# Three matmuls per weight tile into one PSUM half, in place of two into a whole bank

## The reference

```python
h = h + 0.5 * rmsnorm(swiglu(rmsnorm(h, gn[0]), ffn1_w_in[i], ffn1_w_out[i]), gn[1])
hn = rmsnorm(h, gn[2])
m = mixer(hn)            # hgrn2, diff_attention, pool, hgrn2; then hybrid (SSD and attention), recurrent
h = h + rmsnorm(m, gn[3])
h = h + 0.5 * rmsnorm(swiglu(rmsnorm(h, gn[4]), ffn2_w_in[i], ffn2_w_out[i]), gn[5])

def swiglu(x, w_in, w_out):
    g, u = jnp.split(x @ w_in, 2, axis=-1)      # w_in 1024 x 5632, w_out 2816 x 1024
    return (jax.nn.silu(g) * u) @ w_out
```

## Time and profile before

| what | value |
|---|---|
| median of 3 runs (lowest to highest) | 3526.33 us (3525.63 to 3526.66) |
| span of the profiled execution | 3531.6 us |
| profiled span against that median | 5.3 us longer |
| TensorE busy, mean granted clock | 91%, 0.960 |
| VectorE, ScalarE, GpSimd busy | 67%, 52%, 8% |
| HBM read over the span | 151 GB/s |

### The profile page before, as it was taken

How to read it: one execution, slowest core, us unless ns; L and a number is a source line. 1 busy time by engine, 2 the same in 40 slices (tenths; PEclk the granted TensorE clock), 3 DMA queues, 4 the chain that set the end, 5 groups by cost and what they waited for, 6 DMA issues and landing times.

```text
span 3531.6 us, 47236 instructions
## 1 busy us (share of the span) xinstructions
PE 3227.6 (91%) x17800; PEld 2755.1 (78%) x17800; DVE 2375.7 (67%) x2692; ACT 1823.6 (52%) x2180; POOL 268.6 (8%) x184
## 2 busy tenths in 40 slices
PE   8988899998699998799998899999887999997798
PEld 7876788887588887688887678888775788886687
DVE  6767676766576677576766767576765676767675
ACT  4555655554455554555555555555342555555553
POOL 1010101010000001101010010101000101010101
PEclk9998999999899999899999899999997999998899
DMA  5543355554245464355553336455440455553353
GB/s 171 198 136 108 115 183 167 178 190 131 72 157 196 153 194 138 114 179 166 178 192 119 97 130 200 147 187 167 143 155 0 131 187 170 179 191 107 109 193 127
DMA packets 527814, 534.83 MB, mean 151 GB/s; under 512 B 7817, under 2 KB 527116, under 8 KB 527688
## 3 DMA queue, kind: packets, MB, share of 16 engines
q1 hardware_dynamic: 527688, 533.08, 46.5%
HBM read 532.00 MB, written 1.05 MB: 151 GB/s over the span
## 4 chain that ended last, share of the span: by engine, by line
PE 75%; DVE 12%; ACT 9%; DVEq 3%; issue 1%; DMA 0%; SPq 0%; ACTq 0%; POOL 0%; POOLq 0%
PE pp L1992 45%; PE pp L1993 23%; DVE wlo L1826 5%; ACT whi L1718 3%; PE pm L2055 2%; ACT corr L1780 1%; DVEq L515 1%; DVE tsum L1890 0%; ACT L1795 0%; PE pm L2069 0%; DVE mix L518 0%; DVE mix L1923 0%; ACT mix L1747 0%; PE pp L1577 0%; ACT mix L730 0%
## 5 line engine op out<-in xcount | busy, mean ns | idle before, releaser
L1992 PE MATMUL pp<-xs,whi 128*128 128x512 f32 x5824 | 2101.4, 404 | 117.8 <-DVE wlo L1826 92.1
L1993 PE MATMUL pp<-xs,wlo 128*128 128x256 f32 x5824 | 1648.8, 283 | 0.0
L1992 PEld LDWEIGHTS pp<-xs,whi 128*128 128x128 f32 x5824 | 1111.4, 191 | 418.9 <-DVE wlo L1826 78.1
L1826 DVE TENSOR_TENSOR wlo<-raw,whi 128x2048 fp32r<-128x2048 f32 (+2 forms) x455 | 1114.4, 2449 | 214.4 <-ACT whi L1718 214.4
L1993 PEld LDWEIGHTS pp<-xs,wlo 128*128 128x128 f32 x5824 | 1117.4, 192 | 0.4 <-issue 0.2
L1718 ACT ACTIVATE whi<-raw 128x2048 fp32r<-128x2048 f32 (+2 forms) x455 | 926.4, 2036 | 9.0 <-DMA raw<-ffn_w_in 8.7
L1780 ACT ACTIVATE corr<-pp 128x512 f32<-128x512 f32 x468 | 279.0, 596 | 1172.8 <-PE pp L1993 1172.7
L1992 PE MATMUL pp<-hs,whi 128*128 128x512 f32 x2240 | 778.5, 392 | 8.9 <-DVE wlo L1826 7.3
L1993 PE MATMUL pp<-hs,wlo 128*128 128x256 f32 x2240 | 626.1, 280 | 0.0
L1890 DVE TENSOR_TENSOR tsum<-pp,corr 128x512 f32<-128x512 f32 x344 | 237.9, 692 | 435.9 <-ACT corr L1780 434.1
L1694 POOL TENSOR_TENSOR mix<-mix 128x256 f32<-128x256 f32 (+2 forms) x144 | 260.9, 1812 | 3232.5 <-ACT mix L1747 2869.7
(11 more groups left out here) (337 smaller groups left out, 1784.3 us busy)
## 6 DMA issues: line engine op xcount, KB each, us to landing
raw<-ffn_w_in SPq DMA_DIRECT2D x264, 1024.0 KB, 5.1
raw<-ffn_w_out SPq DMA_DIRECT2D x96, 1408.0 KB, 6.2
raw<-hgrn_w_in SPq DMA_DIRECT2D x32, 1024.0 KB, 5.4
raw<-hyb_w_in SPq DMA_DIRECT2D x24, 1024.0 KB, 5.2
raw<-diff_w_in SPq DMA_DIRECT2D x12, 1024.0 KB, 5.2
raw<-hgrn_w_out SPq DMA_DIRECT2D x8, 1024.0 KB, 5.0
raw<-hyb_w_out SPq DMA_DIRECT2D x8, 1024.0 KB, 5.0
raw<-rec_w_in SPq DMA_DIRECT2D x8, 1024.0 KB, 5.7
```

The lines of the kernel that those rows point to most:

```text
L1826: v.tensor_tensor(wlo[:, slot, 0:cols], raw[:, slot, 0:cols], whi[:, slot, 0:cols].bitcast(F32), ALU.subtract).then_inc(sem("weights_lo"), 1)
L1992: mm(bank, whi[:, slot, c:c + P], x[:, x_k, :], start=(k == 0), stop=False)
L1993: return mm(bank[:, 0:T], wlo[:, slot, c:c + P], x[:, x_k, 0:T], start=False, stop=(k == seg.kt - 1))
```

## The change

A new function `three_products` issues three matmuls of 256 columns that all add to the same 256 columns of PSUM: whi x high, whi x low, wlo x high. `tile_product` and the two block products call it. The correction half, `corr`, R_CORR and P_CORR, ScalarE's copies and VectorE's additions are removed; VectorE waits for `panel_done` itself. The multiplication by the norm factor reads PSUM and gives `panel_out`; in the `out` panels and in slot 0 of `down` it is a copy from PSUM, in slot 1 of `down` one addition. In the opening body the wait for the norm factor and the multiplication now stand ahead of the split of slot 0's next weights. The signals `gate_ready`, `hgrn_projected`, `hgrn_values`, `at_keys_in` and `at_values_in` are replaced by counts of `panel_out`. `tsum` (4 KB a partition) becomes `up` (2 KB) and `corr` (4 KB) becomes `group_rstd` (2 KB), which the hybrid mixer uses for a norm factor. The core of the diff:

```diff
 # TensorE
+            def three_products(bank, slot, c, x, first, last):
+                mm(bank, whi[:, slot, c:c + P], x[:, 0:T], start=first, stop=False)
+                mm(bank, whi[:, slot, c:c + P], x[:, T:2 * T], start=False, stop=False)
+                return mm(bank, wlo[:, slot, c:c + P], x[:, 0:T], start=False, stop=last)
             def tile_product(seg, slot, ft, x, k, x_k):
-                bank, c = pp[:, 2 * slot + ft, :], k * PC + ft * P
-                mm(bank, whi[:, slot, c:c + P], x[:, x_k, :], start=(k == 0), stop=False)
-                return mm(bank[:, 0:T], wlo[:, slot, c:c + P], x[:, x_k, 0:T], start=False, stop=(k == seg.kt - 1))
+                return three_products(pp[:, 2 * slot + ft, 0:T], slot, k * PC + ft * P, x[:, x_k, :], k == 0, k == seg.kt - 1)
 # ScalarE, read_out
                         act.wait_ge(sem("panel_done"), g + (slot + 1))
-                        nc.scalar.activation(two(corr[:, slot, :]), corr_half(slot), ACT.Copy).then_inc(sem("corr_copied"), 1)
...
-                                act.wait_ge(sem("gate_ready"), i + (f + 1))
+                                act.wait_ge(sem("panel_out"), g + 1)
 # VectorE, read_out
-                        t = two(tsum[:, slot, :])
-                        y2 = y[:, 2 * i:2 * i + 2, :] if seg.role == "down" else None
-                        if seg.role == "down" and slot == 1:
-                            dve.drain()
-                            dve.wait_ge(sem("corr_copied"), g + 2)
-                            v.tensor_tensor(y2, y2, main_half(slot), ALU.add)
-                            dve.drain()
-                            v.tensor_tensor(y2, y2, two(corr[:, slot, :]), ALU.add).then_inc(sem("panel_out"), 1)
-                        else:
-                            to = y2 if y2 is not None else t
+                        split_now = seg.role in ("down", "out")
+                        dve.wait_ge(sem("panel_done"), g + (slot + 1))
+                        if split_now:
                             if seg.role == "out":
-                                to = y[:, 4 * i + 2 * slot:4 * i + 2 * slot + 2, :]
-                            dve.wait_ge(sem("corr_copied"), g + (slot + 1))
-                            v.tensor_tensor(to, main_half(slot), two(corr[:, slot, :]), ALU.add).then_inc(sem("panel_out"), 1)
-                        wait_rstd = opening and isinstance(i, int) and i == 0 and slot == 0
-                        split_now = seg.role in ("down", "out") or wait_rstd
-                        if nxt and split_now and not (closing and i == seg.bodies - 1 and slot == 1):
-                            split(slot, g + (slot + 3), nxt)
-                        if seg.role in ("down", "out"):
+                                e = v.tensor_copy(y[:, 4 * i + 2 * slot:4 * i + 2 * slot + 2, :], main_half(slot))
+                            elif slot == 0:
+                                e = v.tensor_copy(y[:, 2 * i:2 * i + 2, :], main_half(slot))
+                            else:
+                                dve.drain()
+                                e = v.tensor_tensor(y[:, 2 * i:2 * i + 2, :], y[:, 2 * i:2 * i + 2, :], main_half(slot), ALU.add)
+                            e.then_inc(sem("panel_out"), 1)
+                            if nxt and not (closing and i == seg.bodies - 1 and slot == 1):
+                                split(slot, g + (slot + 3), nxt)
                             continue
-                        dve.drain()
-                        if wait_rstd:
+                        if opening and isinstance(i, int) and i == 0 and slot == 0:
                             dve.wait_ge(sem("rstd_ready"), 2 * s["n"] + 1)
                         if seg.role == "ffn":
                             if slot == 0:
-                                v.tensor_tensor(two(gate[:, :]), t, r2, ALU.mult).then_inc(sem("gate_ready"), 1)
+                                v.tensor_tensor(two(gate[:, :]), main_half(slot), r2, ALU.mult).then_inc(sem("panel_out"), 1)
                             else:
-                                v.tensor_tensor(t, t, r2, ALU.mult)
+                                v.tensor_tensor(two(up[:, :]), main_half(slot), r2, ALU.mult).then_inc(sem("panel_out"), 1)
...
                         if nxt and not split_now:
                             split(slot, g + (slot + 3), nxt)
 # the block products: the same edit, for the recurrent mixer
-                e = nc.scalar.activation(R_CORR[:, half, :], (pp, pm)[slot][:, :, T:2 * T], ACT.Copy)
...
-                v.tensor_tensor(dst[:, k0:k0 + 4, :], (pp, pm)[slot][:, :, 0:T], R_CORR[:, half, :], ALU.add
-                                ).then_inc(sem("rec_read" if n < 2 else "panel_out"), 1)
+                v.tensor_copy(dst[:, k0:k0 + 4, :], (pp, pm)[slot][:, :, 0:T]
+                              ).then_inc(sem("rec_read" if n < 2 else "panel_out"), 1)
```

More of the change, by code:

```diff
@@ L347, in build @@
         SECOND_ORDER = {POOL: (3, 2, 1, 0), REC: (0, 1, 2, 3)}
-        R_GATE, R_X, R_CONV, R_CORR, R_R, R_I, R_A, R_TH = (mix[:, b] for b in range(8))
+        R_GATE, R_X, R_CONV, R_R, R_I, R_A, R_TH = (mix[:, b] for b in range(7))
         def rec_dst(p):
@@ L498, in pe_rec @@
                 for k in range(k0, k0 + 4):
-                    bank = (pp, pm)[slot][:, k - k0, :]
-                    nc.tensor.matmul(bank, whi[:, slot, k * P:(k + 1) * P], xs2[:, k, :], start=True, stop=False)
-                    e = nc.tensor.matmul(bank[:, 0:T], wlo[:, slot, k * P:(k + 1) * P], xs2[:, k, 0:T], start=False, stop=True)
+                    e = three_products((pp, pm)[slot][:, k - k0, 0:T], slot, k * P, xs2[:, k, :], True, True)
                 e.then_inc(sem("rec_quarter" if n < 2 else "panel_done"), 1)
@@ L520, in dve_conv @@
             dve.drain()
-        P_U, P_W1, P_W2, P_RC, P_OUT, P_CORR = (mix[:, b] for b in range(6))
+        P_U, P_W1, P_W2, P_RC, P_OUT = (mix[:, b] for b in range(5))
         def pool_tiles(p):
@@ L541, in act_pool @@
                 act.wait_ge(sem("panel_done"), seg.g0 + slot + 1)
-                nc.scalar.activation(P_CORR[:, 4 * slot:4 * slot + 4, :], (pp, pm)[slot][:, :, T:2 * T], ACT.Copy
-                                     ).then_inc(sem("corr_copied"), 1)
                 if slot == 0:
@@ L615, in pe_pool @@
                 for n in range(4):
-                    bank = (pp, pm)[slot][:, n, :]
                     for t in range(2):
@@ L619, in pe_pool @@
                         k = 2 * (2 * slot + n // 2) + t
-                        nc.tensor.matmul(bank, whi[:, slot, c:c + P], xs2[:, k, :], start=(t == 0), stop=False)
-                        e = nc.tensor.matmul(bank[:, 0:T], wlo[:, slot, c:c + P], xs2[:, k, 0:T], start=False, stop=(t == 1))
+                        e = three_products((pp, pm)[slot][:, n, 0:T], slot, c, xs2[:, k, :], t == 0, t == 1)
                 e.then_inc(sem("panel_done"), 1)
@@ L675, in step @@
                 if name == "turn_values":
-                    pe.wait_ge(sem("at_values_in"), n)
+                    pe.wait_ge(sem("panel_out"), s["segs"][0].g0 + 3 * j + 3)
                     if j:
@@ L682, in step @@
                 elif name.startswith("scores"):
-                    pe.wait_ge(sem("at_keys_in"), n)
+                    pe.wait_ge(sem("panel_out"), s["segs"][0].g0 + 3 * j + 2)
                     if m > 1:
@@ L1130, in step @@
                 if name == "turn":
-                    pe.wait_ge(sem("hgrn_values"), n)
+                    pe.wait_ge(sem("panel_out"), s["segs"][0].g0 + 3 * j + 3)
                     if j >= 2:
@@ new lines, in body @@
+                            v.tensor_tensor(dst[slot], main_half(slot)[:, slot, :], rpre[:, :], ALU.mult).then_inc(sem("panel_out"), 1)
+                        else:
+                            turned, pairs0 = None, 0
+                            if s["kind"] == HGRN:
+                                (kind, pair), pairs0, turned = hg_panel(2 * i + slot), 4 * s["it"], "hgrn_turned"
+                            elif s["kind"] == DIFF:
+                                (kind, pair), turned = at_panel(2 * i + slot), "at_values_turned"
+                            if turned is not None and kind == "v" and pair:
+                                dve.wait_ge(sem(turned), pairs0 + pair)
+                            v.tensor_tensor(dst(2 * i + slot), main_half(slot), r2, ALU.mult).then_inc(sem("panel_out"), 1)
```

59 lines of the change are left out of this document (18 added, 41 removed).

## The result

The changed kernel takes 3567.06 us (median of 4 runs, 3565.55 to 3568.12), the one before 3526.49: the ratio is 1.011, with a 95% interval of 1.0095 to 1.0124. That is 41 us more, where 14 were forecast; it lies inside the range given and on the side forecast, but with another make-up. The profiled executions have spans of 3563.8 and 3531.6 us. Ratios compare fast executions with fast ones; one of e4 (8,173 us) and two of the kernel before that ran beside e1 to e4 (5,155 and 11,063 us) were far slower and are left out.

A forecast was written before the change was run, and what follows sets the result against it. TensorE, 91% busy, was taken as the bound, plus the places where it stands still. Terms 3 + 32 + 41 - 7 - 21 - 6 - 28 = +14 us on 3526.3 gave 3540 us, range 3505 to 3575.

The forecast's parts named there:

- Part 1: Tiles on TensorE: three 256-column slots at 0.117 us each cost about what the old pair did, about +3 us.
- Rival B: Tiles on TensorE: three loaded streams in a row settle at 0.120 us a slot, +73 us, 3613 us; chance 24%.
- Part 2: The 18 sublayer openings: the split behind the norm-factor wait restarts TensorE 2.8 us later, partly absorbed, +32 us.
- Part 3: The 18 openings: the longer TensorE gap drops the granted clock, 2.3 us lost each, +41 us.
- A: Rival at the openings: the clock holds, so its cost vanishes and the time is 3499 us; chance 10%.
- Part 4: Segment change in the FFN, 12 times: without the copy TensorE's wait for the split goes, -7 us.
- Part 5: The 18 sublayer ends: a shorter path to the square gives -21 us, fewer clock drops -6 us.
- Part 6: Inside the mixers: removing the copy and the addition gives -28 us, bounds 10 and 34.
- D: Rival in the mixers: the removed work was hidden behind other steps and gains nothing, 3568 us; chance 8%.
- C: Rival on TensorE's tiles: 256-column slots all run at 0.113 us, 3442 us; chance 11%.
- E: Rival on weight loads: the build leaves out the second load of the same weights; chance 1%.

The follow-up runs named there:

- e4: The changed kernel with 8 more clock-keeping matmuls behind each column sum, so TensorE isn't idle in the opening gap: 3537.64 us, ratio 1.0024.
- e1: The kernel before, with only the 512-column matmul cut into two of 256 in every tile but the first of a sum: 3569.37 us, ratio 1.0116.
- e7: The kernel of e2 with every tile but the first of a sum cut into six matmuls of 128 columns: 9469.64 us in one run.
- e6: The kernel of e2 with a tile's products reordered to whi x high, wlo x high, whi x low: 3502.0 us in one run.
- e2: The changed kernel with the split of slot 0's next weights put back ahead of the opening's wait for the norm factor: 3509.86 us, ratio 0.9949.
- e3: The kernel before, with only the changed kernel's opening order (norm-factor wait and multiplication ahead of slot 0's split): 3583.49 us, ratio 1.0162.
- e12: The kernel of e2 with a VectorE addition of 128x512 and its drain put back in the mixers' 80 head panels: 3538.17 us, ratio 1.0019.
- e11: The kernel of e2 with a ScalarE copy of 128x512 put back in the mixers' 80 head panels: 3536.93 us, ratio 1.0009.
- e8: The kernel of e2, but the FFN keeps two matmuls a tile, correction half, copy and addition except in its last two down panels: 3469.17 us, ratio 0.9838.

## Why the prediction came out as it did

It forecast +14 us and +41 came, +32 between the two spans. That this is inside the range is in part luck, since two misses had opposite signs: by the table the 12 FFNs came out at +63 us where the terms give some +23, and the six mixers at -30 where they give some -9. Point by point:

**Part 1, the tile, failed; it is the main miss.** "I take 0.117, the slot as it runs now." The slot of a 256-column matmul had been read between two others of 512. Three in a row take 0.120 on xs and 0.118 on hs, 0.0076 us more a tile; with 5,824 + 2,240 tiles that is 61 us of TensorE time, where 3 were forecast. e1 shows that the cut alone does it, and that it is paid in the FFNs and not in the mixers. An FFN of the changed kernel has 528 tiles, all of them cut (e1 leaves the first of each sum whole), so it pays 4.0 us, 48 in the twelve. Rival B had this (0.120, 24%) and its argument, "every stream now has a load under it, and the 512 one had room". e7 supports half of that: 128 columns still take 0.111, as if the load set a floor. It doesn't explain the rest, since 0.118 to 0.120 is above both that floor and the streaming of 256 columns. What adds it stays open. e6 excludes the order of the weights, e1 the common columns. The other engines' work is excluded too: in the trace after, xs tiles take 0.360 with VectorE and ScalarE both idle (920 tiles) and with both busy (2,049). The price of a matmul can be stated, not its cause: with the columns unchanged each one added costs 0.0071 to 0.0076 us on xs and 0.0053 to 0.0076 on hs (e2's first trace and the changed kernel's; e1 has 0.0055).

The Trainium skill's page "TensorE: Matmul & The Clock Gate" gives P / 1.2 ns for a weight load of P columns ("LDWEIGHTS (loading the stationary operand)"), by which 128 columns come to an estimate of 107 ns. The 0.111 of e7 at the full clock agrees within 4%. The 0.213 at the lower clock does not, if it is the load that sets the slot there: the slot doubles with the clock, and the formula has no clock in it. The 2.5 ns that the Trainium skill's same page has over the streaming time of a single matmul ("Back-to-back issue gap"), without a budget for its load, is a third of the 7.6 that an added one cost on xs.

**Part 2, the delay at the openings, held.** 2.8 us each were forecast and 2.76 measured in 18 openings. e3, the same order in the kernel before, costs 57 us by the ratio, 52 by the medians and 47 by the spans (delay and clock), with 32 + 41 forecast for the two. In the FFN 1.7 + 2.3 = 4.0 had been the sum; its trace has 3.0 on the mean of 11, and in the mixers 12.5 us for all six, where 12 + 14 had been summed: they hid half.

**Part 3, the clock, held in kind.** It fell behind 18 of 18 gaps. The 7 us stretches behind the openings show 42 us lost (7 x (1 - clock), summed), as forecast, but only 30 were paid by e4 and not 41, 1.7 us an opening. A, that the clock holds, falls with it. Over the whole span the loss hardly grew, from 142 to 148 us ((1 - mean clock) x span): the ends and the mixers got back nearly what the openings lost.

What parts 2 and 3 did not see is that the bank, too, now waits for the norm factor. It stays hidden behind the late split and shows only in e2, as 0.47 us an opening and a lower clock behind some.

**Part 4, the segment change, held**: the idle time ahead of the hs tiles fell by 7.8 us, 7 forecast.

**Part 5, the sublayer's end, held**: 23.2 us shorter over the 18 ends, 21 forecast, and some 3 us more up to the next start, with 6 forecast for the clock.

**Part 6, the mixers, had the right sign and too small a size.** 28 us were taken, with 34 as the upper bound. In e2's trace the mixers are 46.5 us shorter; less 4.4 for their ends (part 5) that is 42. e12 points at the step: "the addition L1890: 18 us, less 12 x 0.7, 9 remain". The chain of waits counts an addition only where it was itself the last to come. In the hybrid's stretch (2480 to 2740 us before) the chain gives 9.5% to VectorE's steps L515 and L518, and an addition that stands in such a run is paid though the chain names other lines. This is a reading and not shown: VectorE is busy for 65% of the hybrid and 73% of the recurrent mixer, and ahead of the hybrid's additions it waited 31 us for the copy, so some of them had room. 80 panels x 0.69 = 55 us would have been the bound. D, that this work was hidden, falls with e11 and e12; that its 3568 us is close to the measured time is chance.

**The sum again.** With what was measured, an FFN comes to tiles 4.0, opening's delay 2.8 less 1.1 (the second split's wait, which is gone), clock there 1.9, segment change -0.7, end -1.3 and the clock behind it -0.4: +5.2, and the table has 5.3. In the mixers the removed work (-42) and the ends (-4) are e2's -46.5, and the late split takes 17 of it back, which leaves the changed kernel's -29.7. Eleven FFNs at 5.3, the first at 4.1 and the mixers make the +32 between the two spans. The +41 between the medians is the same difference: the profiled execution of before lay 5.1 us over its median and that of the changed kernel 3.3 under its own.

C and E fell with the tiles: 0.354 and 0.360 are not 0.339, and 25,896 weight loads stand beside 25,896 matmuls.

## What to carry to other kernels

The price of a matmul slot is to be read from a run of the same slots in a row, or not taken as known: a matmul added with the columns unchanged cost up to 0.0076 us here, which is 2% of a tile, and with 528 of them in each FFN (4.0 us) it outweighed what the copy and the addition gave back there. Remove work where the engine that does it ends the waits (here the mixers and the sublayers' ends) and leave it where TensorE covers it: done in that way, and with the split kept ahead of the norm factor, the edit makes the kernel 1.6% faster instead of 1.1% slower (e8). And when an operand is read later than before, look at everything that stands behind it on that engine: moving one split behind one wait was worth 57 us, of which 30 were clock and not waiting.

## What the runs showed of the hardware

- In e7 a matmul of 128 columns in fp32r with its own weight load takes 0.111 us at the full clock and 0.213 at the lower, where a matmul of 256 columns also takes 0.213. Whether the load or a lower column rate holds it is not settled.
- In e7 the granted clock was at the lower level for most of the run (0.50 from 1000 to 1300 us, mean 0.562), though TensorE issued matmuls of 128 columns without a pause there. The kernel of e2, with 256 columns each, has a mean of 0.965.
- The undisturbed hs tile keeps one mean over a whole stretch of an FFN (174 spacings) and can change it from one FFN to the next in the same kernel: 0.3467 in all 13 stretches with two matmuls; with three, 0.352 in all 13 of e2's first trace, but 0.352 in six, 0.356 in six and 0.360 in one of the changed kernel's. On xs it is 0.360 with three throughout. What picks the value stays open.
- Waits of 4.1 us at the openings (18 of 18, changed kernel and e3) were followed by the lower clock, waits of 1.8 us in 11 and in 7 of 18 (e2's two traces), waits of 1.3 us in none (before). With the same 4.5 us between column sum and restart, but filled so that TensorE idled for 0.7, it stayed at 1.00 in 18 of 18 (e4).
